# Modulation sums in a two-layer diffusion trunk kernel: from columns to rows on four column groups, turned by one product

## The reference, cut to what matters

```python
mod_l = jnp.split((sc @ ada_w[i] + ada_b[i])[:, None, :], N_MOD, axis=-1)   # sc = silu(c), (1, 1024)
sh_m, sc_m, g_m, sh_f, sc_f, g_f = mod_l
h_lat = _modulate(_rms_norm(x, norm_pre_mix[i]), sh_m, sc_m)                # h * (1 + sc_m) + sh_m
x = x + g_m * _rms_norm(y_lat, norm_post_mix[i])
f_lat = _conv_ffn(_modulate(_rms_norm(x, norm_pre_ffn[i]), sh_f, sc_f), ...)
x = x + g_f * _rms_norm(f_lat, norm_post_ffn[i])
```

## Time and profile before

| | us |
|---|---|
| median of 3 runs | 1971.57 (1968.4 to 1972.77) |
| the profiled execution | 1973.64 |
| its span | 1971.9 |
| PE busy | 1927.5 (98%) |
| DVE busy | 1657.2 (84%) |
| POOL busy | 1275.8 (65%) |
| ACT busy | 995.9 (51%) |

### The profile page before, as it was taken

One profiled execution on the slowest core, in us unless ns is written; L12 is line 12 of the kernel. 1 busy time (PEld: TensorE's weight loads), 2 busy tenths in 40 slices (PEclk: granted clock), 3 DMA queues, 4 the chain that ended last, 5 costly groups with the idle time before them and its releaser, 6 DMA issues. The chain is left out here.

```text
span 1971.9 us, 28047 instructions
## 1 busy us (share of the span) xinstructions
PE 1927.5 (98%) x8838; PEld 1577.2 (80%) x8838; DVE 1657.2 (84%) x1745; ACT 995.9 (51%) x1425; POOL 1275.8 (65%) x857
## 2 busy tenths in 40 slices
PE   5999999999999999999999999999999999999998
PEld 3777776888888888888888789878888888888886
DVE  4588888978689898899889886897888888888887
ACT  5767768456544444444444455663434334334334
POOL 4444234575877788977788985475567655656765
PEclk9999999999999999999999999999999999999999
DMA  8322322540223322223232241111111111111114
GB/s 331 101 93 85 121 85 86 203 171 33 86 86 96 96 85 96 81 89 96 85 96 95 70 176 43 66 64 47 61 53 53 58 49 64 55 52 64 52 54 171
DMA packets 78017, 179.76 MB, mean 91 GB/s; under 512 B 5104, under 2 KB 28944, under 8 KB 77328
## 3 DMA queue, kind: packets, MB, share of 16 engines
q1 hardware_dynamic: 77968, 179.13, 26.7%
HBM read 166.52 MB, written 12.58 MB: 91 GB/s over the span
## 5 line engine op out<-in xcount | busy, mean ns | idle before, releaser
L2302 POOL TENSOR_TENSOR So_lo<-So_raw,So_hi 128x512 fp32r<-128x512 f32 x120 | 198.9, 1665 | 199.6 <-DVE So_raw L2939 168.4
L3003 DVE TENSOR_TENSOR Y<-Y,ps 128x1024 f32<-128x1024 f32 x280 | 324.3, 1211 | 3.2
L1820 ACT ACTIVATE So_hi<-So_raw 128x512 fp32r<-128x512 f32 x180 | 112.4, 624 | 147.3 <-POOL So_raw L2294 74.8
L2072 POOL TENSOR_TENSOR red<-red,E_quad 128x512 f32<-128x512 f32 x77 | 125.0, 1623 | 60.4 <-ACT E_quad L1874 57.5
L1820 ACT ACTIVATE WB_hi<-rawB 128x512 fp32r<-128x512 f32 x120 | 74.6, 629 | 166.9 <-PE ps L1243 112.7
L2025 POOL TENSOR_TENSOR WA_lo<-rawA,WA_hi 128x1024 fp32r<-128x1024 f32 x20 | 58.0, 2898 | 145.1 <-DVE u L2632 104.2
L1820 ACT ACTIVATE WA_hi<-rawA 128x512 fp32r<-128x512 f32 x120 | 73.1, 625 | 122.5 <-PE ps L1263 83.4
L1243 PE MATMUL ps<-T_hi,So_hi 128*128 128x512 f32 x336 | 131.3, 391 | 0.0
L1243 PE MATMUL ps<-T_hi,So_lo 128*128 128x512 f32 x336 | 130.8, 389 | 0.0
L1243 PE MATMUL ps<-T_lo,So_hi 128*128 128x512 f32 x336 | 130.7, 389 | 0.0
L1243 PE MATMUL ps<-H_hi,WA_hi 128*128 128x512 f32 x336 | 130.7, 389 | 0.0
(11 more groups left out here) (448 smaller groups left out, 6284.1 us busy)
## 6 DMA issues: line engine op xcount, KB each, us to landing
rawA<-wA SPq DMA_DIRECT2D x62, 512.0 KB, 3.3
rawB<-wB SPq DMA_DIRECT2D x62, 512.0 KB, 3.3
E_quad<-ada SPq DMA_DIRECT2D x44, 512.0 KB, 3.5
quad<-ada SPq DMA_DIRECT2D x8, 2048.0 KB, 9.4
rawB<-wC SPq DMA_DIRECT2D x22, 512.0 KB, 3.7
rawA<-wC SPq DMA_DIRECT2D x20, 512.0 KB, 3.7
ada_first<-ada SPq DMA_DIRECT2D x8, 1024.0 KB, 15.8
outT<-X SPq DMA_DIRECT2D x16, 512.0 KB, 2.7
```

Source lines behind the costliest of these rows:

```text
L1820: A(dst[:, at:at + HF], op_source(name), ACT.Copy).then_inc(op_hi, 1)
L2072: TT(red[:], red[:], E_quad[:, :, k % 2 * P:k % 2 * P + P], ALU.add).then_inc(red_made, 1)
L2302: TT(lo[:, at:at + HF], op_source(name), hi[:, at:at + HF].bitcast(F32), ALU.subtract)\
L3003: TT(at, at, ps[:, bank:bank + 2, :], ALU.add).then_inc(d_added, 1)
```

## The change

The sum over partitions is now made the other way round. The stationary operand is a column of ones repeated 32 times, the moving one is red[:, i], 128 columns. The result is unit i as a row, the same in 32 partitions. The four units of a set go to PSUM partitions 0 to 31, 32 to 63, 64 to 95 and 96 to 127, one 32-column group of the array each (`sum_rows`). `ada_direct` does the same with sc repeated 32 times as the stationary operand and the weights as the moving one, on groups 2 and 3; groups 0 and 1 of this set are units 48 and 49, whose sums move here out of `cols_and_second` (now `count_columns`). So there are 20 sets.

DVE adds each set into a tile mod_rows (128 x 128): a scalar_tensor_tensor with a selector column that is one in partition q of each group, so that set q lands in partitions q, 32 + q, 64 + q, 96 + q (`add_rows`). One product of mod_rows with the identity (`turn_rows`) turns all of them to columns. There are two: one after the heads, at (m, k) = (1, 4) of the output product, from which the first layer's coefficients come (they stood ahead of the scans of the last head), and one in `down_last(0)` after tile 9, which waits for DVE's last `add_rows`; `later_coefs` moves from DVE's tile 9 to tile 10. Set sums and turns are both read from PSUM.

The tile of ones (128 x 128) becomes mod_rows; where ones were used, a single column is broadcast by a zero step, as the moving operand in the sums of squares too.

The diff, cut to its core:

```diff
-            def ada_direct(out):
+            def ada_direct(bank):
 
                 pe.wait_ge(e_full, 32)
                 pe.wait_ge(e1_full, 32)
-                for i, tile in enumerate((E, E_first)):
-                    for k in range(KT):
-                        mm = pe.matmul(out[:, i:i + 1], tile[:, k], silu_c[:, k, 0:1], start=k == 0, stop=k == KT - 1)
-                mm.then_inc(ada_out, 1)
+                for k in range(KT):
+                    for g, tile in ((2, E), (3, E_first)):
+                        pe.matmul(ps[32 * g:32 * g + 32, bank, 0:P], silu_c[:, k, 0:1].to_broadcast([P, 32]), tile[:, k],
+                                  start=k == 0, stop=k == KT - 1)
+                sum_rows(4 * NH + 2, bank, 2)
...
-            def ada_columns(n_red, n, out):
+            def sum_rows(n_red, bank, n=4):
 
                 pe.wait_ge(red_made, n_red)
                 for i in range(n):
-                    mm = pe.matmul(out[:, i:i + 1], red[:, i], ones[:, 0:1], start=True, stop=True)
+                    mm = pe.matmul(ps[32 * i:32 * i + 32, bank, 0:P], one.to_broadcast([P, 32]), red[:, i],
+                                   start=True, stop=True)
                 mm.then_inc(ada_out, 1)
...
+            def turn_rows(n_added, bank):
+
+                pe.wait_ge(ada_added, n_added)
+                pe.matmul(ps[:, bank, P:2 * P], mod_rows[:], ident[:], start=True, stop=True).then_inc(ada_out, 1)
...
                 for t in range(4):
                     mm = pe.matmul(out[:, t * w:t * w + w], src[:, at + t * P:at + t * P + P],
-                                   ones[:, 0:w], start=first and t == 0, stop=last and t == 3)
+                                   one.to_broadcast([P, w]), start=first and t == 0, stop=last and t == 3)
...
                     if (m, k) == (1, 1):
                         pe.wait_ge(y_evac, KT)
-                        ada_columns(4 * NH, 4, ps[:, 7, 0:4])
+                        sum_rows(4 * NH, 7)
                     if (m, k) == (1, 3):
                         square_sums(1, 0)
+                    if (m, k) == (1, 4):
+                        turn_rows(NH + 1, 7)
...
                     if n == 8 and L == 0:
-                        quad_columns(PAIRS + 1, ps[:, 3, 0:4])
+                        sum_rows(rows_added(PAIRS + 1, 7), 3)
+                    if n == 9 and L == 0:
+                        turn_rows(NH + 4 + PAIRS, 3)
...
-            def add_ada_bias(out, first, n, count):
+            def add_rows(bank, chosen, count):
 
                 dve.wait_ge(ada_out, count)
-                TT(M[:, bass.ds(first, n)], out, col("ada_b", first, n), ALU.add).then_inc(ada_added, 1)
+                dve.wait_ge(ada_added, count - 1)
+                STT(mod_rows[:], ps[:, bank, 0:P], chosen, mod_rows[:], ALU.mult, ALU.add).then_inc(ada_added, 1)
...
                     if n == 9 and L == 0:
+                        add_rows(3, sel[:, NH + PAIRS + 1:NH + PAIRS + 2], NH + 4 + PAIRS)
+                    if n == 10 and L == 0:
                         later_coefs()
```

More of the change, by code:

```diff
@@ L116, in build_trunk @@
         ident = sb("ident", [P, P])
-        ones = sb("ones", [P, P])
-        eps = sb("eps", [P, 1])
+        mod_rows = sb("mod_rows", [P, P])
+        const = sb("const", [P, 2])
+        eps, one = const[:, 0:1], const[:, 1:2]
         rms = sb("rms", [P, KT])
@@ L844, in first_context @@
                 mm.then_inc(left_rec, 1)
-            def ada_columns(n_red, n, out):
+            def sum_rows(n_red, bank, n=4):
                 pe.wait_ge(red_made, n_red)
                 for i in range(n):
-                    mm = pe.matmul(out[:, i:i + 1], red[:, i], ones[:, 0:1], start=True, stop=True)
+                    mm = pe.matmul(ps[32 * i:32 * i + 32, bank, 0:P], one.to_broadcast([P, 32]), red[:, i],
+                                   start=True, stop=True)
                 mm.then_inc(ada_out, 1)
-            def quad_columns(q, out):
-                pe.wait_ge(red_made, rows_added(q, 7))
-                for i in range(4):
-                    mm = pe.matmul(out[:, i:i + 1], red[:, i], ones[:, 0:1], start=True, stop=True)
-                mm.then_inc(ada_out, 1)
+            def turn_rows(n_added, bank):
+                pe.wait_ge(ada_added, n_added)
+                pe.matmul(ps[:, bank, P:2 * P], mod_rows[:], ident[:], start=True, stop=True).then_inc(ada_out, 1)
             def column_sums(q, h, src, at, first, last):
@@ L985, in _ @@
             for t in range(2):
-                mm = pe.matmul(ps[:, 5, t:t + 1], ctx_sq[:, 0, t * P:t * P + P], ones[:, 0:1],
+                mm = pe.matmul(ps[:, 5, t:t + 1], ctx_sq[:, 0, t * P:t * P + P], one,
                                start=True, stop=True)
@@ L1326, in ffn @@
                     pe.wait_ge(u_evac, 2)
-                    ada_direct(ps[:, 3, 0:2])
+                    ada_direct(3)
                 down(L, 0)
@@ L2107, in _ @@
             pool.memset(silu_pad[:], 0.0).then_inc(memset_done, 1)
-            pool.memset(ones[:], 1.0).then_inc(memset_done, 1)
-            pool.memset(eps[:], EPS).then_inc(memset_done, 1)
+            pool.memset(mod_rows[:], 0.0)
+            pool.memset(one, 1.0).then_inc(memset_done, 1)
+            pool.memset(eps, EPS).then_inc(memset_done, 1)
             pool.memset(s_exp[:], 0.0).then_inc(memset_done, 1)
@@ L2484, in ada_quad, with add_ada_bias, of @@
                         STT(red[:], rows, s_k, total, ALU.mult, ALU.add).then_inc(red_made, 4)
-            def add_ada_bias(out, first, n, count):
+            def add_rows(bank, chosen, count):
                 dve.wait_ge(ada_out, count)
-                TT(M[:, bass.ds(first, n)], out, col("ada_b", first, n), ALU.add).then_inc(ada_added, 1)
+                dve.wait_ge(ada_added, count - 1)
+                STT(mod_rows[:], ps[:, bank, 0:P], chosen, mod_rows[:], ALU.mult, ALU.add).then_inc(ada_added, 1)
+            def add_ada_bias(bank, first, q0, n, count):
+                dve.wait_ge(ada_out, count)
+                def of(t):
+                    return t.rearrange("p (q u) -> p q u", u=4)
+                made = ps[:, bank, P:2 * P].rearrange("p (u q) -> p q u", u=4)[:, q0:q0 + n // 4]
+                TT(of(M[:, first:first + n]), made, of(col("ada_b", first, n)), ALU.add).then_inc(ada_added, 1)
             def coefs(i, L, ffn_part):
```

50 lines of the change are left out of this document (24 added, 26 removed).

## The result

The changed kernel is **slower by 0.2%**: median 1975.74 us (1972.13 to 1976.73, 9 runs) against 1972.58 us (1968.4 to 1975.07, 9 runs) of the kernel before, ratio 1.002 with a 95% interval of 1.0011 to 1.0029. The forecast was 1966.1 us with a range of 1962.2 to 1970.2. The kernel before has here nine runs and a median 1.0 us above that of the three runs that the forecast was carried to; that part of the distance between 1966.1 and 1975.74 is not the change's.

A forecast was written before the change was run, and what follows sets the result against it. PE, busy 98% of the span, was taken as the bound. The terms summed to 5.4 us saved: 1973.64 profiled becomes 1968.2, and with the runs' median 2.07 lower, 1966.1 us; range 1962.2 to 1970.2.

The forecast's parts named there:

- Price of a group: PE's four sums of a set: 0.81 us before, 0.48 after with overlapping column groups, so a group saves 0.33.
- rival B: Column groups do not overlap, short passes are bound by issue: 1.13 us a group, 6.4 slower, 1978.0 us; chance 0.07.
- Term 1: Heads 1 to 7: saves 1.1 us, not 2.3, since unit B waits for the GeLU; DVE's add is off this chain.
- Term 6: First FFN's loop: ten groups save 3.3 us; PE waits for nothing, and DVE's longer add is covered by a later wait.
- Rival D: The loop gives its 3.3 us back because DVE, or POOL with `red`, becomes the pace: 1969.4 us; chance 0.08.
- Term 4: `ada_direct`: 4.48 us becomes 2.2, PE then waits 0.3 for DVE at `down`'s third tile; net 2.0 saved.
- Term 5: Clock at `ada_direct`: 128-column passes should no longer bring it down to 1.2 GHz; saves 2.3 us.
- Term 7: `down_last(0)`: the turn after tile 9 waits for DVE's add, so the squares come later; 2.5 us lost.
- Term 8: `down_last(0)`: that wait leaves PE idle 4 us and the clock falls behind it; 1.2 us lost.
- Term 2: Output product, (1, 1) and (1, 4): a group saves 0.33 us, a turn costs 0.3; net 0.
- Term 3: Units 48 and 49: four passes gone, 0.45 us saved.
- Term 9: Zero-step column as moving operand in the sums of squares: costs 0.

The follow-up runs named there:

- run 2: Changed kernel, but in heads 1 to 7 VectorE adds the rows before it convolves instead of behind it; median 1973.76 us, ratio to before 1.0006.
- run 3: Kernel before, old PE sums kept, with one more VectorE instruction (a sum over 128 columns) ahead of its bias add in heads 1 to 6; 1973.85 us.
- Run 8: Two runs of the changed kernel, in the first FFN's loop: GpSimd's adds cut to one column, 1964.12 us; ScalarE's scalings cut to one column instead, 1976.77 us.
- e13: Changed kernel, but GpSimd's seven adds per set in the first FFN's loop take one column of each tile instead of 128; 1964.12 us.

## Why the prediction was wrong

**Price of a group: right.** 0.44 instead of the forecast 0.48, so 0.37 saved where 0.33 was forecast; column groups overlap, rival B is out. The terms hold too: 0.09 lost on the way in (forecast 0.13), and 0.35 for the passes and the way out (0.22 and 0.13). On the way out the trace shows 0.22 from the last four starts to the next product, where the first four took 0.13.

**Term 1, heads: the step that failed is "DVE is not on this chain".** I took the GeLU's start from PE's own gates a chain earlier. That chain exists, and run 2, where PE waits 0.1 for it, shows its length: 34.18, in the forecast's range of 34.13 to 34.28. But there is a second one, as late as the first already before (within 0.1 us), and I did not look for it: VectorE's `convolve`, the add, product and scan, `combine`; ScalarE's functions and GeLU; ScalarE's `u` of the next head, for which `convolve` waits. VectorE has at most 0.2 us of idle time in a row between `convolve` and `combine`, and it is not waiting for another engine there. The add is 0.2 longer on that chain, which then takes 34.44, and PE's saving lies where PE waits. Runs 2 and 3 show both halves. Forecast 1.1 gained, 1.3 lost: 0.46 up to head 2, 0.40 in heads 3 to 7, 0.46 behind head 7.

**Term 6, loop: the step that failed is "it is covered".** The cover was not there: the add behind it, said to wait for PE's "22", started at 624.04 without a wait. And I asked only whether VectorE's next instruction is delayed, not who waits for the bank that the add reads: PE's tile at 624.38 before, 622.00 after. Its slack of 0.26 us was less than shorter sums (0.37) and a longer read (0.19) take. Behind it stands a second error: "PE waits for nothing there" gives no slack of the others. Two rows of before would have: VectorE is busy 53.11 us in a period of the first layer's loop and 47.78 in one of the second's, with 55 instructions in each.

```profile
619.35:677.58 58.23, 58.23 (x262) 48.12 (x261) 53.11 (x55) 26.84 (x42) 47.99 (x33) 1.00 0.29 90
1444.00:1501.13 57.13, 57.13 (x254) 47.32 (x253) 47.78 (x55) 22.09 (x34) 35.07 (x26) 1.00 0.17 55
```

Run 8 shows that GpSimd's adds make the difference. Rival D (0.08) was this case: forecast 3.3 gained, 0.1 lost over the ten pairs. Its argument against, that PE waits for nothing, was true of the old sums only.

**Terms 4 and 5: mechanism right, the wait mis-sized.** The product was 0.3 cheaper than thought and the clock stayed up, in this and in eleven more traces. But the 2.3 us taken for the clock were the price in one execution of before: of three more traces with the old sums two lost half as much time at the lower level and one none. The wait was 1.42, not 0.3: I kept VectorE where it had been (free at 483.22), but its last addition ran beside GpSimd (1.76 instead of 0.68), and it started 0.9 late, by the lag. An end time of another engine from the old trace is not a bound of the new one.

**Terms 7 and 8: the wait right, the clock mis-sized.** The last group's 0.36 is lost again in the wait, as forecast. PE idle 3.74, forecast 4. Tile 10 to the gates' spread took 8.40 us (1145.62 to 1154.02) where the same instructions took 4.56 (3.19 from 1146.29 to 1149.48, and 1.37 for tile 10): 3.8 for the clock, forecast 1.2. I had taken a slow stretch of eight passes; this one held sums and a spread too, and ran on for ten us. It is also the longest of eight such traces, and the trace of before is the one of four that kept the clock here: in part the forecast met a bad draw. With 3.39 us of idle time ahead of the turn the clock stayed up in run `e13`:

```profile
1136.75 0.49 PE L860 MATMUL ps<-ident,mod_rows 128*128 128x128 f32 x2 [3.39 <-DVE mod_rows L2497]
1132.00:1144.00 12.00, 8.61 (x47) 7.05 (x46) 8.86 (x21) 4.79 (x10) 5.37 (x5) 1.00 0.82 330
```

From tile 9 to the second layer's squares the lag grew by 2.0 us there. What decides how long the clock stays down is open; the idle time alone does not.

**Terms 2, 3 and 9: right.** The output product and units 48 and 49 gave 0.66 where 0.45 was forecast; eight 128-column passes of squares take 1.13 us with the zero-step operand (at 1264.01) and took 1.13 without (at 1259.86), so nothing was lost on it.

Of the 8.5 us between forecast and trace (-5.4 and +3.1), heads make 2.4, the loop 3.4, `ada_direct` and `down` 1.2, `down_last` 2.3; the output product gave 0.2 more than forecast, and start and end together, which are not the change's, gave 0.6.

## What to carry to other kernels

When work moves off the busiest engine onto another, follow the moved instruction's output and its input: who waits for the result, and who waits for the buffer that it reads. Place it where that engine idles, which here was worth 0.45%, nearly 9 us, between two orders of the same instructions (ratios to before 1.002 and 0.9975). And compare a stage with a sister stage that lacks the suspect: an engine whose time per instruction is longer there may be held up by another. A trace is one execution: where the clock can fall, read a place in several traces before putting a price on it.

## What was not expected of the hardware

- Moving the tiles by 64 or 96 bytes made a kernel 14 or 28 us slower (1985.91 and 1999.48 against about 1972, one run each), with the same instructions but for six short sets.
- One 128-column product on a 32-column group costs PE as much as four on four groups (0.33 and 0.35 us).
- The first 512-column pass after any gap or short product takes 0.33 to the next start, not 0.227, so a wait costs 0.11 more than its length.
- The granted clock behind a gap of PE is not a property of the gap. Ahead of the squares 1.26 us of idle time were followed by no change and 1.22 by 3.4 us at 1.2 GHz, with the same instructions; 1.59 by 3.4 us in one kernel and by none in another; 3.4 to 3.9 us ahead of the turn by 0, 3.4, 6.8 or 10.2 us.
- At `ada_direct` the clock fell without any idle time of PE, during 32 one-column passes or just behind them, in three of four traces.
